# First norm tile by tile, a third weight slot with the residual parked in DRAM, the embedding projection behind the experts, and sixteen straight blocks

## The reference

```python
def decoder_layer(x, p, pool_past, shift_past, wkv_past, pos0, lp):
    h = rmsnorm(x, lp['norm_mix'])
    proj = h @ lp['w_in']                        # 1024 x 4352
    u, z, gate_a, gate_b = ...                   # its columns
    y_a, pool_new = pool_mixer(u, ...)           # trailing means over 2, 4, 8, 16 rows
    y_b, shift_new, wkv_new = rwkv7_mixer(z, ...)  # 8 heads of 64, a matrix state each
    merged = sigmoid(gate_a) * (y_a @ w_branch_a) + sigmoid(gate_b) * (y_b @ w_branch_b)
    x = x + merged @ w_out
    h = rmsnorm(x, lp['norm_ffn'])
    x = x + hier_moe(h, ...)                     # top 1 of 4 groups, then top 2 of its 8 experts
    h = rmsnorm(x, lp['norm_ple'])
    ple = sigmoid(h @ w_ple_gate) * (p @ w_ple_proj)   # p: 256 numbers a row
    x = x + ple                                  # then rmsnorm with norm_final gives y
```

## Time and profile before

| | |
|---|---|
| three runs | 980.85, 983.16, 984.45 us; median 983.16 |
| the profiled execution | 982.39 us, of which 980.6 are its span |
| PE busy | 840.6 us, 86% of the span |
| DVE, ACT, POOL busy | 335.4, 170.3, 113.8 us |
| moved by DMA | 165.89 MB, mean 169 GB/s |
| mean granted clock of PE | 0.928 |

### The profile page before, as it was taken

How to read it: one execution, slowest core, us unless ns; L and a number is a source line. 1 busy time by engine, 2 the same in 40 slices (tenths; PEclk the granted TensorE clock), 3 DMA queues, 4 the chain that set the end, 5 groups by cost and what they waited for, 6 DMA issues and landing times. The chain is left out here.

```text
span 980.6 us, 11072 instructions
## 1 busy us (share of the span) xinstructions
PE 840.6 (86%) x4591; PEld 532.1 (54%) x4591; DVE 335.4 (34%) x564; ACT 170.3 (17%) x300; POOL 113.8 (12%) x166
## 2 busy tenths in 40 slices
PE   2998999999989888989999796798787869753996
PEld 2886888788878775677844253333232323222442
DVE  3226666596014332354311245111010101004444
ACT  3214220000023300230001112111001010112244
POOL 0001464100200213100000000210101010000000
PEclk9999999999989977799999988899898999885998
DMA  9121222223310110125320097499999999965001
GB/s 271 50 66 43 65 65 86 66 72 118 98 44 3 36 32 22 39 74 220 107 66 1 0 391 305 162 407 419 422 419 420 419 421 417 382 264 184 0 24 67
DMA packets 69676, 165.89 MB, mean 169 GB/s; under 512 B 7802, under 2 KB 47942, under 8 KB 57205
## 3 DMA queue, kind: packets, MB, share of 16 engines
q1 hardware_dynamic: 63581, 151.44, 41.0%
q0 software_dynamic: 6048, 13.77, 4.7%
HBM read 155.34 MB, written 17.90 MB: 177 GB/s over the span
## 5 line engine op out<-in xcount | busy, mean ns | idle before, releaser
L890 PE MATMUL PB<-hT,ring 128*128 128x272 f32 x1088 | 256.8, 398 | 0.0
L890 PEld LDWEIGHTS PB<-hT,ring 128*128 128x128 f32 x1088 | 209.1, 193 | 44.5 <-DVE pooled L790 0.3
L1769 PE MATMUL PB<-wexp,BIG 128*64 128x512 f32 x512 | 132.0, 674 | 39.2 <-DMA wexp<-in_expert_up 25.8
L1769 PEld LDWEIGHTS PB<-wexp,BIG 128*64 128x64 f32 x512 | 45.6, 154 | 114.6 <-issue 114.4
L1610 DVE TENSOR_TENSOR BIG<-BIG,PB 128x256 f32<-128x256 f32 x16 | 6.7, 421 | 212.5 <-ACT BIG L1431 212.5
L890 PE MATMUL PB<-pooled,ring 128*128 128x272 f32 x256 | 60.2, 393 | 0.9 <-DVE pooled L799 0.9
L1791 PE MATMUL PQ<-wexp,BIG 128*64 128x512 f32 x256 | 58.4, 598 | 1.2 <-ACT BIG L1435 1.2
L1840 PE MATMUL PQ<-wexp,mhT 128*128 128x512 f32 x128 | 57.5, 610 | 0.0
L1124 PE MATMUL PQ<-ARBK,merged 128*128 128x512 f32 x128 | 55.2, 593 | 1.6 <-DVE merged L806 1.6
L890 PEld LDWEIGHTS PB<-pooled,ring 128*128 128x128 f32 x256 | 48.6, 190 | 11.2 <-DVE pooled L799 1.3
L1124 PEld LDWEIGHTS PQ<-ARBK,merged 128*128 128x128 f32 x128 | 24.2, 190 | 32.2 <-issue 30.1
(11 more groups left out here) (359 smaller groups left out, 956.2 us busy)
## 6 DMA issues: line engine op xcount, KB each, us to landing
wexp<-in_expert_gate SPq DMA_DIRECT2D x16, 2048.0 KB, 17.1
wexp<-in_expert_up SPq DMA_DIRECT2D x16, 2048.0 KB, 24.4
wexp<-in_expert_down SPq DMA_DIRECT2D x16, 2048.0 KB, 25.7
ring<-in_w_in SPq DMA_DIRECT2D x34, 512.0 KB, 4.1
BIG<-in_x_prompt SPq DMA_DIRECT2D x8, 512.0 KB, 11.5
ARBK<-in_w_out SPq DMA_DIRECT2D x1, 4096.0 KB, 13.7
hd<-BIG SPq DMA_DIRECT2D x8, 512.0 KB, 4.9
wexp<-in_w_ple_gate SPq DMA_DIRECT2D x1, 4096.0 KB, 13.2
```

Source lines behind the costliest of these rows:

```text
L890: last = pe.matmul(PB[n % 2][:, h, 0:HT], w, x[:, h * HT:(h + 1) * HT], start=(k == 0), stop=(k == len(ops) - 1))
L1769: last = pe.matmul(bank[2][64 * e:64 * e + 64, :].rearrange("p (q f) -> p q f", q=2), xgT[x][:, k, 64 * e:64 * e + 64], gu, start=(k == 0) ...
```

## The change

- **First norm.** The identity alone (64 KB) is loaded ahead of x, the gain after tile 0, the first unit of weights after x, and only then the other constants and vectors. ACT takes a first square root of nothing needed, to have the table. Squares, root, reciprocal, scaling and turning go by tile, with the takes of tile n-1 behind the scaling of tile n. The turns of the vectors and of the shift state move behind PE's first product.
- **Third weight slot.** `NW` is 3. The third slot lies in the lower part of `BIG`. The residual `X1` is stored to `xd` in DRAM before the weights are loaded, and comes back as `X2` in the third slot after down(14). The buffers of a block's rows move to where X1 was.
- **Embeddings.** Loading, turning and projection of the embeddings leave the mixer and the routing. They are loaded after down(14), and PE and ACT work on them after block 15. ACT's copies stand ahead of the squares of the tail.
- **Sixteen blocks unrolled.** The loops become straight code; gathers and scatters take their indices from `idxT` directly. Overflow blocks get a serial loop of their own, one block a turn, behind the sixteen. w_ple_gate is loaded after down(13).

```diff
 mixer, SP:
-        sp.dma_start(cst[:, :], a["consts"]).then_inc(consts_loaded, 16)
+        sp.dma_start(cst[:, 0:P], a["consts"][:, 0:P]).then_inc(identity_loaded, 16)
         for n in range(NTILE):
             sp.dma_start(xt[0:ROWS[n], n, :], src).then_inc(x_loaded[n], 16)
-        sp.dma_start(gmix[:, :], ...).then_inc(gain_loaded, 16)
+            if n == 0:
+                sp.dma_start(gmix[:, :], ...).then_inc(gain_loaded, 16)
...
+        load_unit(0)
+        sp.dma_start(cst[:, P:], a["consts"][:, P:]).then_inc(consts_loaded, 16)
...
-        sp.wait_ge(merged_ready, KD)
-        emb = load_embeddings(sp, a, BIG, embeddings_loaded)
 mixer, ACT:
+        nc.scalar.activation(ss[:, :], ss[:, :], ACT.Sqrt).then_inc(table_warm, 1)
+        act.wait_ge(table_warm, 1)
+        def root(n):
+            act.wait_ge(mean_square_ready, n + 1)
+            nc.scalar.activation(ss[0:ROWS[n], n:n + 1], ss[0:ROWS[n], n:n + 1], ACT.Sqrt).then_inc(root_ready, 1)
         for n in range(NTILE):
             act.wait_ge(x_loaded[n], 16)
             nc.scalar.activation(..., ACT.Square, accum_out=ss[0:ROWS[n], n:n + 1]).then_inc(squares_summed, 1)
-        act.wait_ge(mean_square_ready, 1)
-        nc.scalar.activation(ss[:, :], ss[:, :], ACT.Sqrt).then_inc(root_ready, 1)
+            if n:
+                root(n - 1)
+        root(NTILE - 1)
 mixer, DVE:
+        dve.wait_ge(gain_loaded, 16)
...
+        scale_tile(0)
+        for n in range(1, NTILE):
+            scale_tile(n)
+            take_turned(n - 1)
+        take_turned(NTILE - 1)
 mixer, PE:
-        pe.wait_ge(consts_loaded, 16)
-        pe.wait_ge(vectors_loaded, 16 * 9)
-        pe.transpose(bank[4][:, 0:46], rows[:, :], ident[0:46, 0:46]).then_inc(vectors_turned, 1)
+        pe.wait_ge(identity_loaded, 16)
...
         for n in range(N0):
+            if n == 1:
+                (the turns of the vectors and of the shift state, with their waits)
 experts:
-UP = 4
-NW = 2
+NG = 4
+NW = 3
...
+    slots = [wexp[:, 0:SLOT], wexp[:, SLOT:2 * SLOT], BIG[:, 0:SLOT]]
+    X2 = slots[2][:, 0:NTILE * D].rearrange("p (n d) -> p n d", n=NTILE)
+    xd = nc.dram_tensor("xd", (T, D), F32, kind="Internal").ap()
 experts, SP:
+        for n in range(NTILE):
+            sp.dma_start(tile_rows(xd, n), X1[0:ROWS[n], n, :]).then_inc(S["residual_parked"], 16)
+        for b in range(2):
+            load_gate_up(sp, b, b, gate_up_loaded[b])
+            load_down(sp, b, b, down_loaded[b])
+        sp.wait_ge(S["x_stored"], 16 * NCHOICE)
+        sp.wait_ge(S["residual_parked"], 16 * NTILE)
+        sp.wait_ge(S["x_turned"], 2 * NTILE)
+        load_gate_up(sp, 2, 2, gate_up_loaded[2])
+        load_down(sp, 2, 2, down_loaded[2])
         for b in range(NW, E_PAIRS + 1):
             if b < E_PAIRS:
-                sp.wait_ge(S["gate_up_ready"], b - NW + 3)
+                sp.wait_ge(S["gate_up_ready"], b - NW + 1)
...
-        sp.wait_ge(S["block_ready"], UP * last_turn + UP - 1)
+        sp.wait_ge(S["block_ready"], E_PAIRS - 2)
         sp.dma_start(WG, ...).then_inc(S["gate_weights_loaded"], 16)
-        sp.wait_ge(S["block_ready"], UP * n_turns)
+        sp.wait_ge(S["block_ready"], E_PAIRS - 1)
+        (five loads of pin, wproj, five loads of X2 from xd)
         sp.dma_start(gf, ...).then_inc(S["final_gain_loaded"], 16)
+        extra = sp.value_load(inb[0:1, :], min_val=0, max_val=NOV)
+        sp.wait_ge(S["block_ready"], E_PAIRS)
+        with sp.If(extra > 0):
+            (the loads of overflow blocks, one at a time)
 experts, POOL:
+        for b in range(NG):
+            gather(b, idxT[:, b:b + 1], rows_gathered[b])
+        for b in range(E_PAIRS):
+            if b + NG < E_PAIRS:
+                pool.wait_ge(S["rows_turned"], b + 1)
+                gather(b % NG, idxT[:, b + NG:b + NG + 1], rows_gathered[b % NG])
+            pool.wait_ge(S["block_taken"], b + 1)
+            store(b % 2, idxT[:, b:b + 1], rows_stored[b % 2])
 experts, ACT:
+        for b in range(E_PAIRS):
+            sigm(b)
+            if b:
+                take_y(b - 1)
+            take_hidT(b)
+        take_y(E_PAIRS - 1)
...
+        act.wait_ge(rows_stored[0], 16 * (E_PAIRS // 2))
+        with act.If(extra > 0):
+            ...
+        for n in range(NTILE):
+            take_embedding(n)
+        for g in range(2 * NTILE):
+            take_projection(g)
         for n in range(NTILE):
             act.wait_ge(S["row_added"], 2 * n + 2)
 experts, DVE:
+        dve.wait_ge(S["residual_parked"], 16 * NTILE)
+        take_x(0)
+        for b in range(E_PAIRS):
+            swiglu(b)
+            if b + 1 < E_PAIRS:
+                take_x(b + 1)
...
+        dve.wait_ge(S["residual_fetched"], 16 * NTILE)
 experts, PE:
+        turn(0)
+        for b in range(E_PAIRS):
+            gate_up(b)
+            if b + 1 < E_PAIRS:
+                turn(b + 1)
+            if b:
+                down(b - 1)
+            turn_hidden(b)
+        down(E_PAIRS - 1)
...
+        pe.wait_ge(S["extra_y_taken"], extra + 1)
+        pe.wait_ge(S["embeddings_loaded"], 16 * (NTILE + 1))
+        (five turns of the embeddings, the ten halves of their projection)
```

More of the change, by code:

```diff
@@ L1252, in experts @@
+    gf = slots[2][:, 8448:9472]
+    pT = slots[2][:, 9472:9472 + 2 * T].rearrange("p (k t) -> p k t", k=2)
+    PP = [slots[1][:, KD * D + D * n:KD * D + D * n + D] for n in range(4)] + [slots[2][:, 10560:10560 + D]]
     cst, wr, gffn, gple, bias = kept
@@ L1382, in _ @@
-        for k in range(UP):
-            gather(k, k)
-        with pool.Fori(0, last_turn) as i:
-            for k in range(UP):
-                gather(UP * i + k + UP, k)
-                store(UP * i + k, k % 2)
-        for k in range(UP):
-            store(UP * last_turn + k, k % 2)
+        for b in range(NG):
[6 more added lines that the diff above has]
+            store(b % 2, idxT[:, b:b + 1], rows_stored[b % 2])
@@ L1795, in _ @@
-        gate_up(0, 0, 0, 32)
-        turn(1, 1, 16)
-        turn_hidden(0, 0)
-        def step(i, k, more, first=False):
-            b = UP * i + k
-            gate_up(b, k % 2, k % NW, 32 * (i * (UP // NW) + k // NW + 1))
-            if more:
-                turn(b + 1, (k + 1) % UP, 16 * (i + (k + 1) // UP + 1))
-            down(b - 1, (k + 1) % 2, (k - 1) % NW, 16 * (i * (UP // NW) + (k - 1) // NW + 1), first)
-            turn_hidden(b, k % 2)
-        for k in range(1, UP + 1):
-            step(0, k, True, first=(k <= NW))
@@ L1816, in turn_normed @@
+        pe.wait_ge(S["emb_projection_taken"], 2 * NTILE - 5)
+        for k in range(2):
+            for g in range(2 * NTILE - 2, 2 * NTILE):
+                last = pe.matmul(projected(g), pT[:, k, NPR:T], wproj[:, k, 512 * (g % 2):512 * (g % 2) + 512], start=(k == 0), stop=(k == 1))
+        last.then_inc(S["emb_projected"], 2)
         def turn_normed(n):
```

492 lines of the change are left out of this document (237 added, 255 removed).

## The result

The changed kernel takes 976.08 us (median of 13 runs, 971.93 to 978.98), the kernel before beside it 982.31 (13 runs, 976.13 to 987.31). The ratio is 0.9941, 95% interval 0.9921 to 0.9962: 6 us or 0.6% faster, where 19 us were forecast, so just over the 0.5% that I called the least that can be told. The profiled execution took 972.55 us, 970.7 of it span, 3.5 less than the median, so the two profiled spans differ by 9.9 us and not by 6. In one later kernel, turn_second_warm, the profiled execution took 1121.73 us at a lower granted clock, 0.731, so it is left out of the median and its stages are not shown.

A forecast was written before the change was run, and what follows sets the result against it. The expert stage was taken as bound by weight transfer, with one large hole; head -5.0, routing and stream -17.4 and tail +3.2 sum to -19.2 us, giving 963.5 us, range 955 to 975.

The forecast's parts named there:

- A, head: First norm up to PE's first products: reordered loads and per-tile norming save 5.0 us, bounds -6.3 to -2.2.
- B, stream: Routing and expert weight stream up to block 15's gate-up product: -17.4 us, bounds -21 to -13.
- S: Start of block 15's gate-and-up product, 855.28 us before the change; the forecast's time origin for the tail.
- Parking's 5.3 us: Before the weight stream: storing the residual to DRAM, 2.2 MB, takes 5.3 us at 420 GB/s.
- the hole: Weight transfer gap at 606 to 629.6 us, DMA share 0.22, with both slots full and block 0 not computed.
- Rival 2: Routing: first gather stuck behind filled slots, landing only at 626, gu(0) 9 us later; total 972.5; chance 0.08.
- Rival 4: Expert blocks: straight code's instruction fetches through full engines cost 68 us, total 1031; chance 0.04.
- Rival 5: Expert blocks: third slot gains nothing, as pitch follows PE's order, not bytes; total 981; chance 0.03.
- C, tail: From block 15's gate-up product to the end: the moved embedding work adds 3.2 us.
- 16 + 4 matmuls take 8.8 us and 1.7 more: Tail: PE's embedding projection takes 8.8 us plus 1.7 for PE having stood idle, before ACT's first square.
- The bounds (-1 to +9.7): Tail: -1 us if the added work is wholly hidden, +9.7 if embeddings land only at S + 32.
- Rival 1: Tail: w_ple_proj lands only with the residual, ACT's squares start at S + 46; total 970; chance 0.13.

The follow-up runs named there:

- turn_second_warm: Changed kernel with embeddings fetched earlier, w_ple_gate behind two result fetches, reordered tail takes, and idle PE matmuls in the head; ratios 0.9689 and 0.9704 to the kernel before.
- head_only: The kernel before with only the head part of the change (identity first, each tile normed as it lands); ratio 0.9946 to the kernel before.
- late_third: Changed kernel, but the third weight slot's first load waits for the end of the first gate-up product; ratio 1.0037 to the kernel before.
- park_twice: Changed kernel, but the residual is stored to DRAM twice, 2.2 MB more, ahead of the first expert weights; ratio 0.9986 to the kernel before.
- half_projection: Changed kernel with only the first of two 128-row halves of the embedding projection; ratio 0.9836 to the kernel before.
- early: Changed kernel with embeddings and w_ple_proj fetched ahead of w_ple_gate, and ACT's wait for block 14's scatter only for overflow blocks; ratio 0.9809 to the kernel before.

## Why the prediction was right or wrong

The forecast was 963.5, in 955 to 975; the kernel takes 976.1. (The one profiled execution, 972.55 us, would have lain inside.)

**A, head: within its bounds.** The first product starts at 21.88 (said 21 to 22, and 27.71 in the earlier trace rows), in part by errors that cancel: tile 1 landed late (its square starts at 8.14), so the first scale ended at 10.4 and not 8.9, but each further tile took DVE 2.5 us and not 2.8. Head_only as a whole gave the forecast's 5 us. But "PE stays the bound up to the next stage, so the gain carries" left out PE's pace: the first group takes 9.0 to 10.5 us against some 7.5, and the profiles show 3.7 us.

**B, stream: right in the main.** -16.2 and -14.8 in two profiles against -17.4. S was forecast "at about 833" and is 833.85. The gather's landing is 8.4 us (said 9.7), no stretch of DMA of 10 us or more is under 1.00 until S. late_third gives 12.5 to 13.9 us of it to the third slot (said 15.0 and 2.0). Parking's 5.3 us of transfer are real by park_twice, but the hole didn't cover them as said: the third slot was full only 3.5 to 4.9 us after gate-up 0. Rivals 2, 4 and 5 fell: the gather wasn't stuck (three full slots lay in SP's queue, the landing took 8.4 us), a block keeps its 16.6 us once the lead is spent, and the slot does what it says. The Trainium skill (DMA: Bandwidth & Descriptors, Queues, rings and completion order), which the forecast cites, says that each DMA engine takes its queues in turn, a packet from each; this trace agrees, with a landing of 8.4 us where some 19 us of data were queued by the forecast's count. Whether straight code saved anything can't be seen under a stream bound by bytes.

**C, tail: wrong, and this is the miss.** The failed step is "16 + 4 matmuls take 8.8 us and 1.7 more". It rests on the earlier trace rows, one row of 16 records in 7.13 us, which I took for 16 matmuls and the whole of eight groups. A float32 matmul leaves two records here, as the 32 of a first group show for its 16. The row was one of two (the other starts at 591.90 and takes 7.03), and stood for half of the work: 17.3 us measured, not 10.5, so 6.8 too few. (The 1.7 us for a slow start were about right: the first row of 8 records takes 5.14 us, the next ones 3.60.) The inputs came 2.4 us after the forecast's S + 24.5: w_ple_proj, issued at 846.88 behind the 4.2 MB of w_ple_gate, was awaited until 860.77, 13.9 us. The turns were quicker than said, so the projection started 1.4 us late, at S + 29.9. With the 6.8 that makes the first square 8.2 us late, at S + 48.4. The bounds (-1 to +9.7) varied only the landing of the inputs, never the length of the work itself. Rival 1 named nearly the right place, the first square at S + 46, for a reason that these runs don't bear out as the main one (w_ple_proj behind the residual): half_projection leaves the loads alone and wins the time back. Its price, 6.5 us, near the 8.4 that are missing, is luck.

Three sums of part C don't come out of their own terms. Inputs at S + 32 would have meant 3.2 + 7.5 = +10.7 and not +9.7; rival 1's S + 46 is 5.8 us behind S + 40.2 and not 6.5; and 4.2 + 1.6 + 2.2 + 0.5 MB with two scatters of 0.5 are 9.5 MB and not 9.1, 1 us more, and the first row add is 1.0 us late. None of them moves the forecast itself.

**The sum.** 12.6 us are missing: 8.4 in the tail, 1.2 in the stream (2.6 by the second profile), 1.3 in the head by the means; the last 1.7 lie within the spread of the arrival, which the range had no term for. The range ended 1.1 us short. The 13 runs of the changed kernel lie within 971.93 to 978.98 us, and a range built on one profile of the kernel before should have been wider by some 3 us either way.

## What to carry to other kernels

Before pricing work by one row, count the whole of it: sum the row's records over the line, and check how many records one operation leaves, for a float32 matmul here two. Work moved onto the chain at the end costs whatever of its length lies behind the wait that the chain has anyway, so its inputs should be fetched early; here the tail grew by 11.6 us with the projection's inputs behind w_ple_gate, and by 1.5 in early, with them ahead and ACT's wait gone. And an order that starts one product sooner can starve the next: look at who waits behind the moved instruction on each engine.

## What the runs showed of the hardware

- PE pauses behind its 1465th matmul record in all sixteen profiles whose stages are shown: 1.7 to 3.3 us where 233 records of small matmuls, 17 to 20 ns each, stand right before the place, 0.2 to 0.5 where the 62 records of idle matmuls at the start leave 171 of them. Idle instructions at the start can so change the time 280 us later.
- Behind the pause the granted clock, 1.00 before it, reads 0.50 to 0.81 (284 to 290 us) in the thirteen profiles with the long pause, and in one of the three with the short one.
- After PE has only turned tiles with rests between them, its first products take 684 ns in place of 392 even where the granted clock reads 1.00 (head_only); the changed kernel's reads 0.73 there, between the two levels of 1.2 and 2.4 GHz.
- Unchanged code between 40 and 560 us differs by 6 us from profile to profile, in short stretches of small matmuls: 74 records take 4.2 us at a granted clock of 1.00 and 6.8 at 0.57.
- A first gather behind queues full of weights lands in 8.4 us, on drained ones in 4.3; from the arrival to S nothing of it shows (278.7 to 280.1 us, and 279.3 with a landing of 6.2).
